# A hybrid SSD / sparse-attention / PEER layer: SSD work placed among the input projections, six gather buffers until step 120, and one piece of query weights kept

## The reference

```
proj = x @ w_in                       # 1024 -> 5184: z, xbc, dt, q, six k/v groups, gates
y_ssd  = ssd_mixer(z, xbc, dt)        # causal conv + silu, 16 heads, 2 chunks of 128, gate, RMS norm
y_attn = nsa_mixer(q, k.., v.., gates)  # compressed blocks (MLP 2048 -> 256 -> 64), selected blocks, window
h = LN(2^0.25 * x + concat(y_ssd, norm(y_attn)) @ w_out)
q = h @ w_query                       # 8 heads x 2 halves x 128; keys: 128 per half
16 of 128 x 128 experts per head by product-key top-k; softmax over the 16 scores
y = sum_k gate_k * gelu(h . u_k) * v_k   # per token, 8 heads x 16 experts
out = LN(2^0.25 * h + y)
```

## Time and profile before

| | us |
|---|---|
| median of 3 runs | 1000.81 (999.88 to 1002.53) |
| profiled execution | 1004.08 |
| its span, first to last instruction | 1002.2 |
| TensorE busy | 785.8 (78%) |
| VectorE busy | 590.8 (59%) |
| ScalarE busy | 428.1 (43%) |
| GpSimd busy | 295.1 (29%) |

### The profile page before, as it was taken

The page is one execution under the profiler, slowest core; times in us unless marked ns, Lnnn a source line. Parts: engine busy times, 40 slices in busy tenths (PEclk is TensorE's granted clock), DMA queues, the critical chain, the costliest instruction groups (busy, mean ns, idle before and its releaser), DMA issues.

```text
span 1002.2 us, 11086 instructions
## 1 busy us (share of the span) xinstructions
PE 785.8 (78%) x3722; PEld 339.5 (34%) x3722; DVE 590.8 (59%) x1401; ACT 428.1 (43%) x1186; POOL 295.1 (29%) x294
## 2 busy tenths in 40 slices
PE   7999999889778798997968476686776666666774
PEld 6876646646344343443312122121221111111110
DVE  2513004862347987877666657578666776767554
ACT  1120115464134896786433343345434434344333
POOL 0020001020023453343433333435444343444320
PEclk9999999979896898797979687878877776777665
DMA  6334466002659999999999999999999999999992
GB/s 253 158 114 174 176 264 248 1 1 84 252 196 420 420 420 420 400 422 421 422 421 425 419 422 420 423 421 420 421 421 420 421 422 420 422 420 421 422 420 113
DMA packets 44776, 335.27 MB, mean 335 GB/s; under 512 B 5936, under 2 KB 5936, under 8 KB 8112
## 3 DMA queue, kind: packets, MB, share of 16 engines
q0 software_dynamic: 36864, 268.45, 64.6%
q1 hardware_dynamic: 7856, 66.12, 16.9%
HBM read 333.50 MB, written 1.05 MB: 334 GB/s over the span
## 4 chain that ended last, share of the span: by engine, by line
DMA 43%; PE 36%; DVE 10%; ACT 7%; issue 3%; POOL 1%; DVEq 0%; SPq 0%; POOLq 0%; ACTq 0%
DMA late<-in_uv,eidx 31%; DMA ring<-in_uv,eidx 10%; PE ps L673 8%; PE ps L959 7%; PE ps L665 6%; PE ps L784 3%; PE ps L819 3%; ACT late L1006 3%; DVE late L1571 3%; ACT L1006 3%; DMA wring<-in_wts 2%; DVE ring L1571 2%; PE ps L924 2%; DVE tmp L1249 1%; ACT tmp L1006 1%
## 5 line engine op out<-in xcount | busy, mean ns | idle before, releaser
L1006 ACT ACTIVATE late<-late 128x1 f32<-128x1 f32 (+3 forms) x787 | 221.9, 285 | 343.2 <-DVE late L1571 321.9
L959 PE MATMUL ps<-ring,late 64*64 64x512 f32 x928 | 164.2, 794 | 94.9 <-ACT late L1006 94.1
L959 PE MATMUL ps<-late 64*64 64x512 f32 x960 | 167.4, 788 | 69.5 <-ACT late L1006 67.2
L1663 POOL DMA_INDIRECT late<-in_uv,eidx x120 | 131.2, 1093 | 263.6 <-PE ps L959 171.2
L1571 DVE CUSTOM_DVE_ANT_0 late<-late,x_sb 128x1024 f32<-128x1024 f32 x120 | 147.0, 1225 | 101.2 <-DMA late<-in_uv,eidx 98.9
L1571 DVE CUSTOM_DVE_ANT_0 ring<-ring,x_sb 128x1024 f32<-128x1024 f32 x116 | 142.1, 1225 | 86.8 <-DMA ring<-in_uv,eidx 85.2
L1663 POOL DMA_INDIRECT ring<-in_uv,eidx x116 | 124.2, 1071 | 197.2 <-PE ps L959 186.9
L1006 ACT ACT_TABLE_LOAD x80 | 102.6, 1283 | 15.0 <-PE ps L665 13.1
L959 PEld LDWEIGHTS ps<-ring,late 64*64 64x64 f32 x928 | 29.6, 158 | 196.7 <-ACT late L1006 179.2
L959 PEld LDWEIGHTS ps<-late 64*64 64x64 f32 x960 | 31.7, 159 | 173.1 <-ACT late L1006 150.7
L673 PE MATMUL ps<-wring,tmp 128*128 128x347 f32 (+4 forms) x256 | 84.6, 492 | 0.0
(11 more groups left out here) (202 smaller groups left out, 779.6 us busy)
## 6 DMA issues: line engine op xcount, KB each, us to landing
wring<-in_wts SPq DMA_DIRECT2D x23, 2048.0 KB, 8.6
wring<-in_wts SPq DMA_DIRECT2D x2, 1428.0 KB, 5.9
wring<-in_wts SPq DMA_DIRECT2D x2, 1388.0 KB, 6.9
wring<-in_wts SPq DMA_DIRECT2D x4, 512.0 KB, 7.4
lnw<-in_ln SPq DMA_DIRECT2D x4, 512.0 KB
late<-in_uv,eidx POOLq DMA_INDIRECT x120
ring<-in_uv,eidx POOLq DMA_INDIRECT x116
wring<-in_wts SPq DMA_DIRECT2D x1, 1432.0 KB
```

Of the source, the lines that this page charges most:

```text
L959: last = mm(o[t][n * HD:(n + 1) * HD, :], factor[tokens, :], values[tokens, n * 512:(n + 1) * 512], start=start, stop=stop, skip_group_che ...
L1006: return nc.scalar.activation(out, in_, func, **kw)
L1663: G.indirect_dma_start(row(slots[g]), None, uv, bass.IndirectOffsetOnAxis(eidx[:, u % 2, k:k + 1], 0)).then_inc(row_here[slots[g]], 16)
```

## The change

1. *SSD among the projections.* TensorE's order becomes: xbc, cmp, channel transposes, tm 0, tm 1, decay sums, `cb`/`seg` of chunk 0, tm 2, `yd`/`st`, `cb`/`seg` of chunk 1, tm 3, `yd`/`yo`, tm 4, tm 5, z 0, token transposes of tile 0, z 1, then block MLP and attention woven together, with three quarter pieces of the output projection ahead of the pair loop and three in it (`FILL`). The other engines' orders follow; ScalarE's three Silu calls on the conv output stand directly behind the cmp copies, ahead of all `tm` and `z` copies; the SSD's y is now kept in `x_tm`, `Ma` in `ring3`. VectorE's rope of both tiles stands between chunk 0's outputs and chunk 1's `Ma`.
2. *Hidden layers of keys and values* are computed in turns, the values' output on partitions 64 to 123. The values' weights are no piece any more but are loaded early into `x_sb` and `sk`.
3. *First transfers* in quarters and halves.
4. *Token transposes of tile 1* move from the pair loop to behind the output projection.
5. *Query weights of heads 0 and 1* (`kept`) are loaded once into `ring3` and serve both tiles; row buffers 6 and 7 (`ring3`) join at step 120.
6. *The first choice* (`choose_first`) gives the first eight expert indices before it looks for the other eight.

```diff
-RING0 = 8
+GROWTH = [(0, (0, 1, 2, 3, 4, 5)), (120, (6, 7)), (160, (8, 9))]
 RING = 10
-SWITCH = 160
-KT_AT = 6
+FILL = {2: 3, 4: 4, 6: 5}
...
+        Ma = view(0, NH, P, src=ring3)
+        w1v = [home.rearrange("p a n -> p (a n)").rearrange("p (c n) -> p c n", n=CHID) for home in (x_sb[:, :, :], sk[:, :, :])]
...
+        kept = ring3[:, :].rearrange("p (k n) -> p k n", k=KD)
...
-            order += [(18 + n, ("q", i, ...)) for n in range(4)]
+            order += [(18 + n, ("q", i, ...)) for n in range(1, 4)]
...
+                if k == 4:
+                    for half in range(2):
+                        at = starts[13] + half * NT * D
+                        sp.dma_start(w1v[half].rearrange("p c n -> p (c n)"), wts[:, at:at + NT * D]).then_inc(w1v_here, 16)
+                if k == 15:
+                    await_full(sp, "hid", 1)
...
+                if k == 16:
+                    await_full(sp, "S", 0, NU[0] - 1)
+                    sp.wait_ge(k_upper, 1)
+                    sp.dma_start(ring3[:, :], wts[:, starts[18]:starts[19]]).then_inc(kept_here, 16)
...
+            def block_hidden():
+                wt = next_piece()
+                pe.wait_ge(w1v_here, 32)
+                for w in range(2):
+                    pe.wait_ge(X_ready[w], 1)
+                o = [await_free(pe, "hid", w) for w in range(2)]
+                for c in range(CLEN // 2):
+                    for w, weights in enumerate((wt[:, c, :], w1v[c // 8][:, c % 8, :])):
+                        last = mm(o[w][w * HD:w * HD + NKV * NCMP, 0:CHID], Xc[:, w, c, :], weights, start=c == 0, stop=c == CLEN // 2 - 1)
...
+            channel_transposes()
+            tokens("tm", 0, widths[0])
+            tokens("tm", 1, widths[1])
+            decay_sums()
+            chunk_scores(0)
+            tokens("tm", 2, widths[2])
+            chunk_sums(0)
+            chunk_scores(1)
+            tokens("tm", 3, widths[3])
+            chunk_sums(1)
+            tokens("tm", 4, widths[4])
+            tokens("tm", 5, widths[5])
+            tokens("z", 0, 512)
+            token_transposes(0)
+            tokens("z", 1, 512)
+            block_hidden()
+            tokens_here(0)
+            scores(0, 0)
+            block_transposes()
+            scores(0, 1)
+            block_keys()
+            mixer_transposes(0, 0)
+            block_values()
+            scores(0, 2)
+            fill(0)
+            block_key_transposes()
+            fill(1)
             compressed_scores(0)
+            fill(2)
+            compressed_transposes(0)
+            for u in range(NU[0] + 1):
                 if u + AHEAD < NU[0]:
                     scores(0, u + AHEAD)
+                if u < NU[0]:
                     weight_transposes(0, u)
+                if u:
                     values(0, u - 1)
+                if u in FILL:
+                    fill(FILL[u])
+            fill(6)
+            fill(7)
             mixer_transposes(0, 1)
             for m in range(4, 8):
                 mix_part(0, m)
+            token_transposes(1)
             hidden_transposes(0)
...
+            for i in range(NT):
+                chunk_weights(i)
+                chunk_decays(i)
+                chunk_outputs(i)
+                if i == 0:
+                    for tile in range(NT):
+                        rope(tile)
+            for i in range(NT):
+                ssd_gate(i)
...
             for g in range(NT * STEPS):
                 if k == 0:
-                    pool.wait_ge(idx_ready, u + 1)
-                if g == SWITCH:
-                    await_full(pool, "q", NT - 1, 3)
+                    pool.wait_ge(idx_ready, u + 1 + (u > 0))
+                elif g == TOPK // 2:
+                    pool.wait_ge(idx_ready, 2)
+                if g == GROWTH[1][0]:
+                    await_full(pool, "q", 1, 0)
+                if g == GROWTH[2][0]:
+                    await_full(pool, "q", 1, 3)
```

More of the change, by code:

```diff
@@ L234, in bank_plan, with tokens, chunk_scores @@
     rotate("BT")
-    rotate("acs")
-    for i in range(NT):
+    def tokens(kind, n):
+        for i in range(NT):
+            rotate(kind, n, i)
+    def chunk_scores(i):
         rotate("cb", i)
@@ L239, in bank_plan, with chunk_sums @@
             rotate("seg", i, n)
[L240 to L243 removed]
+    def chunk_sums(i):
+        for name in ("yd", i), ("yo" if i else "st",):
+            for g in range(NG):
+                rotate(*name, g)
+    tokens("tm", 0)
+    tokens("tm", 1)
+    rotate("acs")
+    chunk_scores(0)
+    tokens("tm", 2)
+    chunk_sums(0)
+    chunk_scores(1)
+    tokens("tm", 3)
+    chunk_sums(1)
+    tokens("tm", 4)
+    tokens("tm", 5)
+    tokens("z", 0)
+    for n in range(2):
+        rotate("qT", 0, n)
+    for b in range(2):
+        rotate("kT", 0, b)
+    tokens("z", 1)
     def in_turn(banks, *names):
@@ L517, in row @@
             return home[:, n * 2 * D:(n + 1) * 2 * D]
-        slots = [g % RING0 if g < SWITCH else (g - SWITCH + RING0) % RING for g in range(NT * STEPS)]
+        slots, idle = [], []
+        for g in range(NT * STEPS):
+            for since, more in GROWTH:
+                if g == since:
+                    idle = list(more) + idle
+            slots.append(idle.pop(0))
+            idle.append(slots[-1])
         def arrivals(g):
@@ L731, in _, with tokens, channel_transposes @@
-            for i in range(NT):
+            def tokens(kind, n, width):
+                w = next_piece()
+                for i in range(NT):
+                    o = await_free(pe, kind, n, i)
+                    for k in range(KD):
+                        last = mm(o[:, 0:width], xT_sb[:, k, i * P:(i + 1) * P], w[:, k, :], start=k == 0, stop=k == KD - 1)
+                    filled(last, kind, n, i)
+            def channel_transposes():
+                pe.wait_ge(silu_done, 3)
+                for i in range(NT):
+                    for half in range(2):
+                        o = await_free(pe, "xT", i, half)
+                        for c in range(4):
+                            last = tr(o[:, c * P:(c + 1) * P], xc[:, 4 * half + c, i * P:(i + 1) * P], ident)
+                        filled(last, "xT", i, half)
+                o = await_free(pe, "BT")
+                for g in range(NG):
+                    last = tr(o[:, g * P:(g + 1) * P], xc[:, KD + g, 0:P], ident)
+                filled(last, "BT")
@@ L732, in _, with decay_sums, chunk_scores @@
+            def decay_sums():
+                pe.wait_ge(a_ready, 1)
+                o = await_free(pe, "acs")
+                for i in range(NT):
+                    for n, m in enumerate((tri, strict)):
+                        at = (2 * i + n) * NH
+                        last = mm(o[:, at:at + NH], m, a_sb[:, i, :], start=True, stop=True)
+                filled(last, "acs")
+            def chunk_scores(i):
                 cols = slice(i * P, (i + 1) * P)
@@ L813, in query_part @@
                         await_taken(pe, "hT", i, half)
-                    if first == 0:
+                    if piece == 0:
+                        pe.wait_ge(kept_here, 16)
+                        query[0] = kept
+                    elif first == 0:
                         query[0] = next_piece()
@@ L1090, in soft, with query_pairs @@
                 f(gexp, gtop, ACT.Exp, bias=gsm[:, 0:1], accum_out=gsm[:, 1:2]).then_inc(ge_ready, 1)
-            def token_copies(i):
-                for n in range(2 * (i + 1)):
+            def query_pairs(i, pieces):
+                for n in pieces:
                     o = await_full(act, "qT", i, n)
@@ L1272, in _, with rope @@
             heads = lambda ap: ap.rearrange("p (h d) -> p h d", d=HD)
-            dve.wait_ge(c_here, 16)
-            for i in range(NT):
+            def rope(i):
                 for n in range(3):
@@ L1316, in statistics, with block_values_apart @@
+            def block_values_apart():
+                o = await_full(dve, "vc")
+                for kv in range(NKV):
+                    last = tt(Vbd[:, kv, :, :], bc(o[:, kv * HD:(kv + 1) * HD], 1, GQ), bc(cst[:, C_HEAD:C_HEAD + GQ], 2, HD), ALU.mult)
+                taken(last, "vc")
             def statistics(src, half, at):
@@ L1368, in _ @@
                     await_taken(dve, "acs")
+                    for w in range(2):
+                        dve.wait_ge(X_ready[w], 1)
                     tt(heads(xdd), heads(xdt), bc(ea[:, 0, 1, :], 2, HD), ALU.mult).then_inc(xdd_ready, 1)
@@ L1551, in _ @@
                 first_norm(0, part)
-            for part in range(len(CHOOSE_STEPS)):
-                choose(0, 0, part)
+            choose_first()
             def finish(i, part):
```

431 lines of the change are left out of this document (225 added, 206 removed).

## The result

The changed kernel takes **1010.41 us** in the median of 4 runs (1007.97 to 1011.32), the kernel before beside it 1000.35 (4 runs, 999.66 to 1002.53): ratio **1.0092 [1.0071, 1.0113]**, slower. The forecast was 999.1 us, with a range of 990 to 1008. Its sign was wrong.

The account below looks back on a forecast made before the run. TensorE was taken to set the pace up to the first gather, then DMA bytes at about 416 GB/s, then a fixed tail. Terms -0.3 - 3.5 - 2.4 - 5.0 + 9.5 = -1.7 us gave 999.1 us, range 990 to 1008.

Parts of the forecast that it names:

- the kept piece: Gather stage: tile 1's first query piece is not loaded again, 2.1 MB at 416 GB/s, -5.0 us.
- -0.3 - 3.5 - 2.4: Changes before the first gather: up to tile 0's output projection, then clock in the norm and query part, then first choice.
- split choice: Before the first gather: the first eight rows are issued without waiting for the other eight indices, -2.4 us.
- Silu wait: Projections: channel transposes behind the cmp projection wait for ScalarE's copies, table load and three Silu calls, +5.9 us.
- wait for Ma: Projections: tile 1's segment sums wait for VectorE's Ma, which stands behind the rope of both tiles, +8.1 us.
- Moved work: SSD matmuls and tile 0's transposes, placed between the projections, take 27.0 us of TensorE time.
- Clock: Half clock behind each of the two new projection waits, 3.0 us each, +6.0 us (bounds 0 and 8).
- my 54 and 16.0: TensorE work left behind the last projection, 54 us; then the output projection's fourth weight piece and what follows, 16.0 us.
- Query part: After the output projection: transposes in the norm's gap keep the clock up, first query part 3.6 instead of 6.6 us.
- rival (b): Block MLP: the two hidden layers run one after the other, +7.0 us, giving 1006.1 us; chance 0.12.
- the term of the six buffers: Gather stage: six row buffers instead of eight up to step 120 starve the DMA, +9.5 us (bounds 4.4 and 15.6).
- rival (a): Gather stage, steps 15 to 117: six buffers starve the DMA at every burst, 15.6 us, giving 1005.2 us; chance 0.18.

Follow-up runs that it names:

- e1: The changed kernel with eight row buffers from the start and the query weights of heads 0 and 1 loaded for each tile: 994.9 us.
- e2: The kernel before with only six row buffers up to step 120, nothing else of the change: 1018.4 us.
- f5: e1 with both tiles' rope behind chunk 1's Ma and the channel transposes behind the tm 0 pieces: 974.5 us.
- e3: The changed kernel with the rope of both tiles on VectorE behind chunk 1's Ma: 992.5 us.
- h2: The changed kernel, six buffers, query weights of heads 0 and 1 loaded for each tile, rope and channel transposes later: 991.4 us.
- g3: e1 with the two hidden layers of the block MLP in series instead of in turns: 998.4 us.
- e4: The changed kernel, still with six buffers, but the query weights of heads 0 and 1 loaded for each tile: 1010.6 us.
- f6: e4 with six row buffers only until step 64 and eight from there: 1005.3 us.
- f3: e1 without loading the first query piece for tile 1, which uses the weights of heads 2 and 3: 989.1 us.
- f1: e1 with the rope of both tiles on VectorE behind chunk 1's Ma: 981.4 us.

## Why the prediction was wrong

**What held, as a sum: everything but the buffers and the kept piece.** These terms summed to -0.3 - 3.5 - 2.4 = -6.2 us. e1 has just these parts and took 0.9939 [0.9917, 0.9960] of before, -6.1 us [-8.3, -4.0]. That the two agree to 0.1 us is luck, since errors cancel. The first gather came earlier than forecast (by the traces 10.0 us before that of the kernel before, 6.4 before e2's), since the work ahead of the hidden layers was priced too high. Against that the split choice gave nothing that shows in the time, and e1's stage from the first gather to the last landing is 2.5 us longer than before's (698.9 and 696.4), for which I had no term. Inside the sum:
- Start: the first matmul at 5.38 instead of 6.64 us: -1.3 (forecast -1.0).
- Silu wait 6.10 us (5.9), wait for Ma 8.38 us (8.1), both at the place and for the reason forecast.
- Moved work: f5, where only 0.96 us of wait is left, starts its hidden layers at 171.97 us; less 149.2 - 1.26 + 0.96 this makes 23.1 us for the moved pieces. I had 27.0. Half of the difference is the channel transposes, 3.9 us as I read them and 1.96 in f5: the row that I read them from was at half clock, 3.38 us for 16 records that take 1.91 in f5 (the lines below). The rest is spread over the other pieces.
- Clock: 189.87 - (149.2 - 1.26 + 23.1 + 6.10 + 8.38) = 4.4 us for both waits (6.0), but without the second wait e3 was another 3.4 us faster further on, by stretches at full clock that were at half. That was left out, and it is no rule: without both waits f5 has a query part of 5.38 us again, while h2, the same code up to there, has 3.69.
- From the hidden layers to the end of the output projection (251.90 + 7.13 = 259.0): 69.2 us; my 54 and 16.0 make 70.0.
- Query part: 5.28 us, not 3.6; the transposes in the norm's gap did not keep the clock up. Split choice: 2.7 us at the first issue (2.4), nothing seen in the time. The first gather came at 280.6, not 285.5; most of the 5 us are the moved work and the clock.
- The hidden pair: 7.05 us (7.3), rival (b) falls. g3 shows that it is the turns that do it: in series the same 64 take 13.14. Both series use all 128 rows, and the changed kernel's trace has the second series' weight load from 190.35 to 190.48 us inside the first series' matmul from 190.34 to 190.72. The rule of the Trainium skill, "TensorE: Matmul & The Clock Gate", "The mechanism" of Part 3, that a weight load overlaps matmuls only when row groups differ, does not hold here for two tiles that differ by column. What its "TensorEngine Tiling (Array Packing)", "Key Properties", says, that different tiles load and multiply in parallel, is what this trace shows. I could have known it: the eight records of the earlier trace rows hold pairs with the same rows and different columns, and in the trace of before these start 7 ns apart (417.170 and 417.177 us), so it was wrong that no row shows such a pair.

The channel transposes of the kernel before, then of f5:

```profile
168.78 3.38 PE L716 MATMUL ps<-cst,late 128*128 128x128 f32 x16
```

```profile
72.66 1.91 PE L705 MATMUL ps<-cst,late 128*128 128x128 f32 x16
```

**What failed: the term of the six buffers, +9.5 us.** It measures 15.7, 16.9 and 17.3 in three pairs of kernels. The failed step is this one: "Between bursts the lag does shrink, but only by some 0.2 us a step, so I take +9.5 (bounds 4.4 and 15.6)". From the rows I had lateness of 3.3 (row 22), 4.4 and 2.2 (rows 43 and 63), 3.3 (row 115), and 2.4 for the earlier start. By stretches the rows alone are 3.3, 6.6 and 3.3; e4 against e1 has 5.7, 7.8 and 5.1, e2 against before 7.6, 6.3 and 5.0. So the losses do add, each burst in full, as rival (a) said, and the discount I made was unfounded. f6 shows the adding directly: eight buffers in steps 64 to 119 give back that stretch's loss and nothing of the others'. The places were read rightly, too: in e2 the rows 43 and 115 have their dots 5.95 and 5.79 us after their issue, as on an empty queue. My reading of why nothing is made good is that the step's other items come in a fixed order with the rows, so TensorE cannot catch up while the DMA is idle; no run tests this.

Even the upper bound was a little low, and 2.4 us of its 15.6 were put there for the earlier first gather, which e1 and e4 both have; the rows alone gave 13.2, against 15.7 to 17.3. The 10 us hole at 428 us is a burst that the rows of before do not show. It does not explain the gap, since e2 loses as much and in rows 32 to 63 its uses are at most 6.7 us apart. What makes up the rest stays open.

**Why two buffers matter and one does not.** A row takes 2.5 us of the queue, so six buffers hold 15 us of it, seven 17.5, eight 20. A buffer is away for the trip from issue to dot on an empty queue, 5.74 us above, and then until TensorE has done with the row. That leaves 9.3 us from dot to use with six buffers, 11.8 with seven and 14.3 with eight. In the trace of e1 this time is 6.6 us in the mean of the first 120 rows; it is over 9.3 in 15 of them, over 11.8 in 4, and the longest is 12.1. This estimate from rows fits the three counts; only six, seven and eight were run.

**The second failed term: the kept piece, -5.0 us.** It is right in a full queue (f3: -5.9) and was booked against a queue that the same edit empties. With six buffers it measures -0.2 and -2.4. The two parts of one edit were priced separately, each against the kernel before, and the two errors, 6.2 and 4.8 us, are 11.0 of the 11.8 us between the forecast change of -1.7 and the measured +10.1.

By the medians: -6.1 (e1) + 15.7 (e4) - 0.2 = +9.4 us, measured +10.1. Rival (a) was nearest (1005.2), and would have needed the kept piece at nothing to reach 1010.2. Whether the kept piece with six buffers gives nothing or some 3 us stays open.

## What to carry to other kernels

Where the queue of transfers is the bound, price a buffer by its round trip: issue to landing on an empty queue, plus the time from landing until the row has been used, over the time of one transfer. In this kernel six buffers did not cover it, and the losses of the stretches added up; seven nearly did, and the eighth was worth next to nothing. A saving in bytes counted in full here only with a full queue, so price it together with what empties the queue. And look at what an engine carries ahead of a moved piece of work: 7.3 us of rope in front of one small tensor, and three Silu calls with no matmuls to cover them, cost 20 us of this kernel (994.9 and 974.5), and moving two blocks gave them back.

## What the runs showed of the hardware that was not expected

- A wait of TensorE has an after-effect far from it. Removing 7.4 us at 113 us moved the first gather by 13.2 us; the query part 140 us later went from 5.28 to 3.69 us. The seven traces with both waits and the same order show two later stretches at half clock, e3 and f1 neither. It is not a fixed price: with the Silu wait gone too (f5) the first gather moved by 6.2 us for 6.1 us of wait, and the query part took 5.38 us; in h2, the same code up to there, it took 3.69 and the first gather came 1.7 us earlier.
- The same code up to the first gather, kernel before and e2, differs by 3.6 us in one execution each (291.7 and 288.1): in the window from 212.1 to 265.5 us the granted clock was 0.95 and 0.99. A difference of first gathers between two single traces may be no better than this.
- Two series of matmuls on different column halves of the array with the same 128 rows run side by side when issued in turns (64 in 7.05 us) and one after the other, but for the last three records, when issued in series (13.14 us).
